# A fused trunk block on one core: the opening norm in two halves, the first shift's weights in three pieces, rows and partial sums accumulated straight into columns

## What is computed

```python
c_act = jax.nn.silu(c)
mod = c_act @ w_ada[l] + b_ada[l]
shift1, scale1, gate1, shift2, scale2, gate2 = jnp.split(mod, N_MOD, axis=-1)
h = _modulated_norm(x, norm_mix_g[l], shift1, scale1)   # _rmsnorm(x, g) * (1 + scale) + shift
z = h @ w_in[l]
```

## Time and profile before

| what | us |
|---|---|
| median of 3 runs | 1550.87 (1549.7 to 1551.68) |
| the profiled execution's own time | 1550.7 |
| its span, first to last instruction | 1548.6 |
| PE busy in the span | 1523.7 (98%) |
| DVE busy in the span | 1185.3 (77%) |
| ACT busy in the span | 792.0 (51%) |
| granted TensorE clock | 0.999 of full speed |

### The profile page before, as it was taken

How to read it: one execution, slowest core, us unless ns; L and a number is a source line. 1 busy time by engine, 2 the same in 40 slices (tenths; PEclk the granted TensorE clock), 3 DMA queues, 4 the chain that set the end, 5 groups by cost and what they waited for, 6 DMA issues and landing times.

```text
span 1548.6 us, 19442 instructions
## 1 busy us (share of the span) xinstructions
PE 1523.7 (98%) x6856; PEld 1247.8 (81%) x6856; DVE 1185.3 (77%) x1432; ACT 792.0 (51%) x1181; POOL 375.4 (24%) x287
## 2 busy tenths in 40 slices
PE   7999999999999999999999999999999999999998
PEld 4778777788888888888887778888888888888887
DVE  6987988646556684466338999999999987777876
ACT  5368888644554461112124655555555553444447
POOL 0023434422222200000000233333333330233324
PEclk9999999999999999999999999999999999999999
DMA  9431223212332256667211144444444446677722
GB/s 348 176 112 52 89 69 89 85 55 82 110 102 80 96 173 223 191 195 240 96 55 30 53 150 150 150 154 156 153 150 150 150 129 228 220 242 249 254 80 109
DMA packets 199838, 219.54 MB, mean 142 GB/s; under 512 B 8928, under 2 KB 155712, under 8 KB 199104
## 3 DMA queue, kind: packets, MB, share of 16 engines
q1 hardware_dynamic: 199744, 218.32, 42.7%
HBM read 160.61 MB, written 57.67 MB: 141 GB/s over the span
## 4 chain that ended last, share of the span: by engine, by line
PE 76%; DVE 15%; ACT 4%; issue 3%; DMA 1%; POOL 0%; SPq 0%; ACTq 0%; DVEq 0%; POOLq 0%
PE ps L784 53%; PE ps L855 15%; DVE wop L1711 4%; DVE hidw L2220 1%; PE ps L996 1%; PE ps L1087 1%; PE ps L1069 1%; DVE ps L1724 1%; PE ps L940 1%; DVE part_acc L1773 1%; ACT wop L1150 1%; DVE yq L1808 1%; DVE tn L1803 1%; DVE ti L1915 1%; DVE yq L2163 1%
## 5 line engine op out<-in xcount | busy, mean ns | idle before, releaser
L1711 DVE TENSOR_TENSOR wop<-raw,wop 128x512 fp32r<-128x512 f32 (+1 forms) x520 | 378.3, 736 | 166.9 <-ACT wop L1150 164.0
L1150 ACT ACTIVATE wop<-raw 128x512 fp32r<-128x512 f32 (+1 forms) x520 | 293.5, 569 | 405.2 <-PE ps L784 156.7
L784 PE MATMUL ps<-yq,wop 128*128 128x512 f32 x1680 | 405.2, 390 | 1.4 <-DVE wop L1711 1.0
L784 PEld LDWEIGHTS ps<-yq,wop 128*128 128x128 f32 x1680 | 314.3, 188 | 71.2 <-issue 3.8
L628 POOL TENSOR_TENSOR raw<-raw,raw 128x512 f32<-128x512 f32 (+1 forms) x64 | 94.4, 1475 | 879.0 <-DVE wop L1711 635.7
L784 PE MATMUL ps<-dq,wop 128*128 128x512 f32 x840 | 191.4, 389 | 0.6 <-DVE wop L1711 0.5
L784 PEld LDWEIGHTS ps<-dq,wop 128*128 128x128 f32 x840 | 157.4, 188 | 34.3 <-issue 1.4
L784 PE MATMUL ps<-t4q,wop 128*128 128x512 f32 x528 | 128.4, 392 | 2.0 <-DVE ps L1724 1.9
L784 PE MATMUL ps<-t2q,wop 128*128 128x512 f32 x528 | 127.6, 390 | 1.9 <-DVE wop L1711 1.1
L784 PE MATMUL ps<-t3q,wop 128*128 128x512 f32 x528 | 127.8, 391 | 0.8 <-ACT snap_u L1162 0.8
L784 PE MATMUL ps<-t1q,wop 128*128 128x512 f32 x528 | 127.7, 391 | 0.0
(11 more groups left out here) (234 smaller groups left out, 1943.5 us busy)
## 6 DMA issues: line engine op xcount, KB each, us to landing
dq<-hid_keep SPq DMA_DIRECT2D x35, 1024.0 KB, 7.2
raw<-in_w_in SPq DMA_DIRECT2D x96, 256.0 KB, 3.3
raw<-in_w_up SPq DMA_DIRECT2D x96, 256.0 KB, 3.5
hid_keep<-part_b SPq DMA_DIRECT2D x40, 512.0 KB, 3.0
ada_ring<-in_w_ada SPq DMA_DIRECT2D x32, 512.0 KB, 4.5
hid_keep<-part_t SPq DMA_DIRECT2D x20, 512.0 KB, 2.8
raw<-in_w_down SPq DMA_DIRECT2D x80, 128.0 KB, 2.4
ada_w<-in_w_ada SPq DMA_DIRECT2D x8, 1024.0 KB, 11.4
```

Of the source, the lines that this page charges most:

```text
L784: done = nc.tensor.matmul(bank, left[:, w, lk, :], right[:, x, rk, :], start=(first and w == 0 and x == 0), stop=(last and w == 1), skip_g ...
L1150: nc.scalar.activation(wop[n % 4][:, 0, 0:depth[n], :], raw[slot][:, 0:depth[n], :], ACT.Copy).then_inc(f_hi, 1)
L1711: V.tensor_tensor(wop[n % 4][:, 1, 0:kd, :], raw[slot_of[n][0]][:, 0:kd, :], wop[n % 4][:, 0, 0:kd, :].bitcast(F32), ALU.subtract).then_in ...
```

## The change

The kernel's beginning is rewritten; from the units (L784) on it is the same. In words:

- The roots, their inverses, the diagonals, the sum over partitions and the copy of the norm are done for the token blocks 0 to 3 and 4 to 7 apart (`first_root`, `first_diag`, `first_norm`). The first root stands on ACT before the squares of blocks 4 to 7, and the first diagonal on DVE before the copy of block 6.
- `sq0` (the squares' unused output) moves to the tile X, so that the two copies of `rbc0` need not wait for it. `eps_t` is set by GpSimd.
- ACT's Exp for the logarithm moves behind the copies of the norm, and with it a table load. All of the series' steps on DVE that stood before the first `normed` move behind `normed(5)`.
- The first shift's weights come in DMAs of 4, 2 and 2 row blocks instead of 4 and 4. PE takes the row blocks 0, 1 and 6 of it, and DVE 2, 3, 4, 5 and 7.
- `add_row` is gone. `row_and_part` makes each column as an accumulation of two matmuls, one of the copied row and one of `part_acc`, in two lots of two columns each; ACT copies the row in two pieces. The shift's first two columns are ready apart from the other two.
- The first block of the input is split by halves of the tokens (`first_hi`, `first_lo`), and `first_gates` begins with the first half of block 0 for three tiles.
- The orders of ACT and DVE behind it are rewritten, and three `keep_busy` matmuls stand at other places.

The core of the diff:

```diff
-        sq0 = place("sq0", [S], F32, "T", 1 * TILE)
+        sq0 = place("sq0", [S], F32, "X", 7 * TILE)
...
-        PE_ROWS = ((0, 1, 2, 4), (3, 4, 5), (), ())
+        KQ = KH // 2
+        PIECES = [((0, KH), (KH, KT))] * 4
+        PIECES[1] = ((0, KH), (KH, KH + KQ), (KH + KQ, KT))
+        PE_ROWS = ((0, 1, 2, 4), (0, 1, 6), (), ())
...
+            def row_and_part(p, i):
+                pe.wait_ge(row_ready, 2 * p + i + 1)
                 pe.wait_ge(acc_ready, p + 1)
-                nc.tensor.matmul(ROW_IN[p][0:1, 0, :], ones[:, 0:1], part_acc[p][:, :], start=False, stop=True).then_inc(row_sum, 1)
-
-            def row_to_columns(p):
-                pe.wait_ge(row_ready, p + 1)
-                for j in range(KH):
-                    last = nc.tensor.matmul(COLS[:, KH * p + j:KH * p + j + 1], mod_row[0:1, j * P:(j + 1) * P], ones[0:1, 0:1],
-                                            start=True, stop=True)
+                for j in range(KQ * i, KQ * i + KQ):
+                    column = COLS[:, KH * p + j:KH * p + j + 1]
+                    nc.tensor.matmul(column, mod_row[p][0:1, j * P:(j + 1) * P], ones[0:1, 0:1], start=True, stop=False)
+                    last = nc.tensor.matmul(column, part_acc[p][:, j * P:(j + 1) * P], ones[:, 0:1], start=False, stop=True)
...
+            def first_norm(h):
+                pe.wait_ge(x_diag, h + 1)
+                nc.tensor.matmul(ps[1][:, h, :], ones[:, :], diag0[:, HB * h:HB * h + HB, :].rearrange("p b t -> p (b t)"),
+                                 start=True, stop=True).then_inc(x_rbc, 1)
+
+
+            pe.wait_ge(xT_copied[1], COPIER[:7].count(1))
+            first_norm(0)
+            modulation_rows(0, PE_ROWS[0][:2])
+            first_norm(1)
+            modulation_rows(0, PE_ROWS[0][2:]).then_inc(row_sum, 1)
+            pe.wait_ge(xT_copied[1], COPIER.count(1))
             modulation_rows(1, PE_ROWS[1][:1])
+            for i in range(2):
+                row_and_part(0, i)
+            modulation_rows(1, PE_ROWS[1][1:]).then_inc(row_sum, 1)
             pe.wait_ge(param_col, len(ROWS))
-            row_to_columns(0)
-            modulation_rows(1, PE_ROWS[1][1:])
-            add_row(1)
+            keep_busy(1, ada_w[0][:, 0, :])
+            pe.wait_ge(rbc_kept, 2)
             pe.wait_ge(s1_ready, 1)
-            row_to_columns(1)
+            row_and_part(1, 0)
+            keep_busy(1, ada_w[0][:, 0, :])
             pe.wait_ge(shift_ready, 1)
-            keep_busy(2, ada_w[0][:, 0, :])
+            row_and_part(1, 1)
...
-                for k in range(2):
+                for h in range(2):
                     for s in range(3):
-                        gate_tile(s, (k,))
+                        gate_tile(s, (0,), (h,))
+                for s in range(3):
+                    gate_tile(s, (1,))
...
+            def first_root(h):
+                act.wait_ge(x_squared, HB * h + HB)
+                nc.scalar.activation(rs[:, HB * h:HB * h + HB], ss[:, HB * h:HB * h + HB], ACT.Sqrt, bias=epsc, scale=1.0 / D)\
+                    .then_inc(x_root, 1)
...
-                    act.wait_ge(lam_e, 1)
-                    nc.scalar.activation(lt[:, 1, :], lt[:, 0, :], ACT.Exp, scale=-1.0).then_inc(lam_e, 1)
-                    act.wait_ge(eps_made, 1)
+                    act.wait_ge(consts_made, 1)
                     nc.scalar.activation(sd[:, :], epsc, ACT.Sqrt)
-            act.wait_ge(x_squared, NB)
-            nc.scalar.activation(rs[:, :], ss[:, :], ACT.Sqrt, bias=epsc, scale=1.0 / D).then_inc(x_root, 1)
+                    first_root(0)
+            first_root(1)
...
-            act.wait_ge(x_rbc, 1)
-            nc.scalar.activation(rbc0[:, :], flat(ps[1]), ACT.Copy).then_inc(rbc_kept, 1)
+            for h in range(2):
+                act.wait_ge(x_rbc, h + 1)
+                nc.scalar.activation(rbc0[:, H[h]], ps[1][:, h, :], ACT.Copy).then_inc(rbc_kept, 1)
+            act.wait_ge(lam_e, 1)
+            nc.scalar.activation(lt[:, 1, :], lt[:, 0, :], ACT.Exp, scale=-1.0).then_inc(lam_e, 1)
             row_copy(0)
             hi(0)
             row_copy(1)
+            act.wait_ge(tn_ready, 1)
+            act.wait_ge(shift_ready, 1)
+            nc.scalar.activation(b11[:, 0, 0, :], tn[:, 0, H[0]], ACT.Identity, bias=mod[:, 0:1]).then_inc(first_hi, 1)
+            nc.scalar.activation(b12[:, 0, 0, :], tn[:, 0, H[1]], ACT.Identity, bias=mod[:, 0:1]).then_inc(norm_hi, 1)
             hi(1)
-            act.wait_ge(shift_ready, 1)
-            norm_high(0)
             hi(2)
-            for k in range(1, KH):
-                norm_high(k)
+            norm_high(1)
+            act.wait_ge(shift_ready, 2)
+            norm_high(2)
+            norm_high(3)
...
+            def first_diag(h):
+                part = rs[:, HB * h:HB * h + HB]
+                dve.wait_ge(x_root, h + 1)
+                step(V.reciprocal(part, part))
+                V.tensor_tensor(diag0[:, HB * h:HB * h + HB, :], ident[:, :].unsqueeze(1).to_broadcast([P, HB, P]),
+                                part.unsqueeze(2).to_broadcast([P, HB, P]), ALU.mult).then_inc(x_diag, 1)
...
-            log_start()
-            dve.wait_ge(x_root, 1)
-            step(V.reciprocal(rs[:, :], rs[:, :]))
-            V.tensor_tensor(diag0[:, :, :], ident[:, :].unsqueeze(1).to_broadcast([P, NB, P]),
-                            rs[:, :].unsqueeze(2).to_broadcast([P, NB, P]), ALU.mult).then_inc(x_diag, 1)
+            first_diag(1)
             mod_pieces(0, (3, 5, 6, 7))
+            mod_pieces(1, (2, 3, 4, 5))
...
-            mod_pieces(1, (0, 1, 2))
-            log_terms(7, 6)
-            scale_columns(0)
-            mod_pieces(1, (6, 7))
+            dve.wait_ge(param_col, len(ROWS))
+            scale_columns(0, 2)
+            mod_pieces(1, (7,))
             normed(0)
+            mod_columns(1, 3, slice(0, KQ)).then_inc(shift_ready, 1)
             lo(0)
+            dve.wait_ge(shift_ready, 1)
+            dve.wait_ge(first_hi, 1)
+            V.scalar_tensor_tensor(b11[:, 1, 0, :], tn[:, 0, H[0]], mod[:, 0:1], b11[:, 0, 0, :].bitcast(F32),
+                                   ALU.add, ALU.subtract).then_inc(first_lo, 1)
+            lo(1)
...
-            log_terms(5, 4, 3, 2)
+            log_start()
+            log_terms(7, 6, 5, 4, 3, 2)
```

93 lines of the change are left out of this document (47 added, 46 removed).

## The result

| | median, us | runs |
|---|---|---|
| before | 1550.36 (1549.58 to 1551.68) | 7 |
| after | 1555.41 (1554.78 to 1556.38) | 7 |

The ratio is 1.0032, 95% interval 1.0022 to 1.0042: the changed kernel is slower, by about 5 us. The prediction was 1551.8 with a range up to 1553.2, and it gave a chance of 0.07 to a kernel slower by more than 0.2%. It was wrong, and the time lies outside its range.

The account below looks back on a forecast made before the run. PE, busy from 110 us on, bounds the kernel; the change shifts that stretch's start through DVE's work up to PE's third product at 89.85. Terms -0.1 + 1.5 - 0.4 = +1.0 gave 1551.8 us, range 1549.4 to 1553.2.

Parts of the forecast that it names:

- term one: DVE's beginning up to the fourth weight: of a 1.6 us lead 1.5 is spent, leaving -0.1 us.
- The fourth weight starts at 41.8: DVE's fourth weight, `lo(3)`, was to start at 41.8 us instead of 41.93.
- 1.2 us idle: DVE behind the first normed was to stand 1.2 us idle, waiting for the shift's columns until 30.5.
- Two matmuls for each column double it: PE's passes for the scale's four columns: 2.0 us, from 24.9 to 26.9, at a distance of 0.12.
- Rival 3: TensorE at its lower level in the gates, gate matmuls 1.64 times as long: 1555.4 us; chance 0.05.
- unread matmuls still fill the waits: Argument against a slower TensorE in the gates: unread matmuls fill PE's waits for the shift's columns.
- Term two: DVE behind `normed(5)`: 17 series steps instead of eight, nothing hiding them, so +1.5 us.
- Term three: ACT's table load at 75.55 goes; DVE waited only 0.37 us for ACT there, so -0.4, not -1.3.
- Rival 1: Up to 1.4 us of the beginning's lead is still there at the fourth weight: 1550.4 us; chance 0.26.
- Rival 2: Table load before the row copy holds ACT 1.3 us longer, DVE's line slips: +0.8, 1552.6 us; chance 0.07.
- Rival 4: Early root or half norm buys nothing since weight landings at 21.2, 24.0, 26.7 rule; 1552.8 if 1 us late; chance 0.05.

Follow-up runs that it names:

- e6_between: Changed kernel with the shift's row 1 moved between the two lots of the scale's columns, no work added; 1554.26 us, ratio 1.0028.
- e4_before_double: Kernel before with the scale's four columns made twice over, sixteen one-column passes of one kind in a row; 1552.11 us, ratio 1.0016.
- b1_before_accum: Kernel before with the accumulation alone: `add_row` gone for both quarters, each column two accumulated passes; 1555.14 us, ratio 1.0027.
- e5_addrow: Changed kernel with the accumulation undone: `add_row` back, each column one matmul again; 1551.25 us, ratio 1.0005.
- e2_series: Changed kernel with nine of the series' seventeen steps moved from behind `normed(5)` into DVE's wait behind `normed(0)`; 1553.73 us, ratio 1.0024.
- e9_before_load: Kernel before with an unused one-column Exp behind the parameter copies, which takes away the table load at 75.55; 1549.92 us, ratio 0.9996.
- v1: Changed kernel with the accumulation undone and the series spread over three places on DVE (five, two and ten steps); 1550.85 us, ratio 1.0002.
- e1_filler: Changed kernel with one more unread 512-column matmul between the two lots of the scale's columns; 1555.32 us, ratio 1.0035.
- e7: Changed kernel with the shift's row 1 between the scale's lots and nine series steps behind `normed(0)`; 1553.95 us, ratio 1.0026.

## Why the prediction was wrong, point by point

**The failed step is term one**, "The fourth weight starts at 41.8", by 3.1 us (44.88), and in it the wait at the shift's first columns: "1.2 us idle", which measured 3.26. Behind these columns term one held: from them to `lo(3)` lie 11.5 us, against 11.3 in the forecast (41.8 less 30.5). The error lies ahead of them, 33.40 instead of 30.5, in what PE's work up to the columns was said to take: "Two matmuls for each column double it" for the passes, and every row and unread matmul at its price at the upper level. By its own steps, in after:

- The scale's passes start at 25.11, not 24.9 (+0.2).
- A pass of the accumulation takes 0.155, not 0.122: +0.5 for the scale's sixteen, and +0.2 for the shift's first eight (1.17 in e6_between, 1.0 in the forecast). The forecast took the distance of a lot that has one kind of weight, for a lot that alternates two. e4_before_double's sixteen of one kind took 0.12 each and b1's sixteen alternating ones 0.153.
- The unread matmul in front of the shift's passes takes 1.06 at the upper level, not the 0.7 that the forecast gave it (28.7 to 29.4): +0.35.
- The clock: the rows +0.6 (2.31 against 1.71 in e5_addrow), the unread matmul +0.94, the first passes +0.15: +1.7, as e6_between measured by taking the fall away.
- The two rows at the upper level take 1.71, not 1.8: -0.1.

Their sum is 2.85, and the distance is 2.9. So the slower clock is the largest part of the failed step, and the passes' price comes second.

**Rival 3** (TensorE at its lower level) had the right mechanism, at 0.05, with its place in the gates and its cause in PE's gaps. The gates did run slower, 15.49 for 60. But in after they kept nobody waiting: DVE had the columns of part 2 without a wait at 54.86. What cost was the stretch before them, which was on DVE's path, and there the forecast took PE's rows and unread matmuls at their price at the upper level. That the rival's 1555.4 is also the measured time is luck, since its 3.5 us came from 36 gate matmuls that made DVE wait. Its mechanism did cost about 0.6 in e4_before_double and in b1_before_accum. The prediction argued "unread matmuls still fill the waits", that is, that a busy PE keeps its clock. PE was busy at 1.00 in the windows in which the clock fell.

The Trainium skill, "TensorE: Matmul & The Clock Gate", section "What's actually happening", says that a hardware block sets the clock by how busy PE has been. The trace of after does not agree if "busy" is read as the profile's busy share: that is 1.00 at 29 to 32 us, with the clock at 0.50.

**Term two** (+1.5): measured +1.58, and e2_series gave 1.3 of it back. **Term three** (-0.4, not -1.3): measured -0.47, and -0.46 alone in e9_before_load. **Rival 1** (the lead survives) did not come: `normed(0)` was 0.8 ahead and DVE's wait took all. **Rival 2** (the load costs in front of the row copy) did not either. ACT's timeline of after:

```profile
23.16 1.28 ACT L1248 ACT_TABLE_LOAD   x1
24.45 0.21 ACT L1248 ACTIVATE lt<-lt 128x8 f32<-128x8 f32 x1
24.57 0.62 ACT L1219 ACTIVATE mod_row<-ps 1x256 f32<-1x256 f32 x2
```

The Exp starts 0.01 behind the load's end, and the row's two pieces together take 0.62, against 0.59 for the whole one. By the Trainium skill, "ScalarE: Activation LUTs", section "What ACT_TABLE_LOAD costs", a drain of about 1.38 us would stand here; the trace of after has none, nor has that of e9_before_load (22.00 behind 20.71 and 1.28). **Rival 4** (the landings rule): they came as forecast.

**What stays open.** That the accumulation brings the early fall with it is shown: the three traced kernels that have its sixteen passes unbroken fall, e5_addrow and v1 without it do not, and neither does before. What exactly drops the clock is not shown. Sixteen alternating passes and two rows behind them did so in after, e2_series and b1_before_accum, at once; the same with a row or an unread matmul between did not; sixteen passes of one kind did so late or by another cause; and the second fall of after has the same work ahead of it as a stretch of e6_between without one. Each order of the work has one trace, so the chance of a single execution is not ruled out between after and e1_filler or e6_between.

And of the 5.05 us between the medians the beginning explains 4.0. Between the profiled executions, of which that of after is the slowest of its seven, it explains 4.0 of 6.0, and the other 2.0 can be placed. From 1307 us to the start of the last part of the down projection, 0.5 us more pass (it starts at 1516.15 in after and at 1511.64 in before). The last 1.5 are behind the last block that DVE writes: the span ends 5.9 us behind it in after and 4.5 in before, while the last stores land (median 4.0 us from issue to landing, against 3.3). This is not a mark of the change. The 4.5 is also that of e5_addrow and v1, and 5.8 to 6.4 that of all others, e9_before_load among them, which is no slower than before. Whether the executions without a profile have the same two amounts, no run shows.

## What to carry to other kernels

Replacing one matmul of 512 columns by many of one column is not a saving because the columns are few: here `add_row` cost 0.95 us (two passes), and its removal put eight more passes on the path, made all sixteen take 0.155 instead of 0.12, and in these kernels the clock fell behind them. Price work on TensorE at both of its levels wherever the change makes a stretch of tiny matmuls, also where PE shows no idle time, and look at the granted clock window by window. If such passes can't be avoided, try a wide matmul between them that has to be done anyway; in e6_between it kept the clock up and gave 1.7 us back in the trace.

## What the runs showed that I had not expected

- The granted clock fell to 0.50 with PE's busy share at 1.00: in after at 28.8, where PE's last idle time had ended at 18.55, and in b1_before_accum at 29.3, where it had ended at 25.97. It stayed at 1.00 in before where PE was busy for 0.42 of a window (31 to 32).
- One-column passes took 0.12 each with one kind of weight (16 in 1.94 in e4_before_double) and 0.155 where a row of one partition and a block of 128 partitions alternate.
- A fall to 0.50 stands between 59.6 and 64.0 us in e1, e5, e6, e7 and v1, and not in before or after. PE still waited for DVE's weight at the third product (0.19 us in e7, 0.55 in the others), so no cost was seen.
- In v1 one step of the series took 1.29 us instead of 0.17:

```profile
59.39 1.29 DVE L1792 TENSOR_SCALAR lt<-lt 128x8 f32<-128x8 f32 x1
```

It is a step of 8 columns for each partition. Just then, from 59.36 to 60.64, GpSimd adds two tiles of 128x512, and the step ends at 60.68. The same GpSimd instruction stands at 58.18 in before, for 1.29 us, and the split of the input beside it takes 2.03 on DVE instead of 1.28. That the one holds the other is likely from this, but no run varied it.
